# Dealing an expert's third weight matrix to partitions in blocks of four consecutive rows, with a column stride of four in the first product

## The reference

```
def expert_choice_ffn(h, router_w, w1, w3, w2):
    ...
    gate, idx = lax.top_k(aff.T, cap)
    xe = xf[idx]
    hid = jax.nn.silu(jnp.einsum('ecd,edf->ecf', xe, w1)) * jnp.einsum('ecd,edf->ecf', xe, w3)
    ye = jnp.einsum('ecf,efd->ecd', hid, w2) * gate[..., None].astype(h.dtype)
    out = jnp.zeros_like(xf).at[idx.reshape(-1)].add(ye.reshape(-1, D).astype(xf.dtype))
```

## Time and profile before

| | |
|---|---|
| median of 3 runs | 1744.39 us (1741.98 to 1746.46) |
| profiled execution | 1747.4 us |
| its span, first to last instruction | 1745.3 us |
| mean granted TensorE clock over the span | 0.958 |
| PE busy / PEld busy | 1611.5 / 1042.8 us |
| MATMUL at line 1592, both slot sets | 147.4 + 145.4 us busy, 8192 records |
| MATMUL at line 1604, both slot sets | 112.7 + 112.7 us busy, 512 records |

### The profile page before, as it was taken

The page is one execution under the profiler, slowest core; times in us unless marked ns, Lnnn a source line. Parts: engine busy times, 40 slices in busy tenths (PEclk is TensorE's granted clock), DMA queues, the critical chain, the costliest instruction groups (busy, mean ns, idle before and its releaser), DMA issues.

```text
span 1745.3 us, 38027 instructions
## 1 busy us (share of the span) xinstructions
PE 1611.5 (92%) x16782; PEld 1042.8 (60%) x16782; DVE 614.0 (35%) x1286; ACT 430.5 (25%) x726; POOL 248.3 (14%) x251
## 2 busy tenths in 40 slices
PE   5999989999869999999999989888888978999997
PEld 2554435655447677666655467667765546676764
DVE  4543584641520000003149456644463151110110
ACT  3245414530411111103010246432231032100000
POOL 0000000000001111100000036155540001121211
PEclk9999999999989999998999989999899998999998
DMA  9635444031589999973211100011114226999995
GB/s 341 206 129 192 145 151 103 1 145 48 213 309 365 383 389 391 379 284 132 85 61 52 48 1 2 1 51 51 51 51 169 85 109 220 379 379 378 396 388 182
DMA packets 89167, 324.84 MB, mean 186 GB/s; under 512 B 10836, under 2 KB 16584, under 8 KB 80872
## 3 DMA queue, kind: packets, MB, share of 16 engines
q1 hardware_dynamic: 75296, 284.67, 43.1%
q0 software_dynamic: 9456, 32.65, 6.9%
q10 hardware_dynamic: 4312, 6.03, 1.0%
HBM read 301.17 MB, written 22.16 MB: 185 GB/s over the span
## 4 chain that ended last, share of the span: by engine, by line
PE 72%; DVE 6%; DMA 4%; issue 3%; ACT 1%; POOL 0%; POOLq 0%; ACTq 0%; DVEq 0%; SPq 0%
PE pairs L223 19%; PE pairs L1592 15%; PE pairs L1604 12%; PE pairs L1575 2%; PE pairs L1236 2%; PE pairs L345 2%; DMA ring<-in_exp_w 2%; PE pairs L1250 1%; PE pairs L2074 1%; PE pairs L2301 1%; PE pairs L2094 1%; PE pairs L2057 1%; PE pairs L2312 1%; DMA ring<-in_w_mod 1%; PE pairs L734 1%
## 5 line engine op out<-in xcount | busy, mean ns | idle before, releaser
L223 PE MATMUL pairs<-hT,ring 128*128 128x128 f32 (+1 forms) x1120 | 306.1, 435 | 2.2 <-ACT hT L359 2.2
L223 PEld LDWEIGHTS pairs<-hT,ring 128*128 128x128 f32 x1120 | 170.3, 192 | 138.5 <-issue 138.4
L359 ACT ACTIVATE arena<-pairs 128x512 f32<-128x512 f32 (+6 forms) x212 | 124.0, 603 | 393.5 <-PE pairs L223 126.5
L223 PE MATMUL pairs<-ring,hT 128*128 128x512 f32 (+1 forms) x448 | 178.5, 557 | 0.0
L1592 PEld LDWEIGHTS pairs<-arena 128*64 128x64 f32 x4096 | 144.5, 138 | 14.4 <-issue 14.3
L1592 PEld LDWEIGHTS pairs<-arena,ring 128*64 128x64 f32 x4096 | 142.7, 137 | 13.9 <-issue 13.9
L1592 PE MATMUL pairs<-arena 128*64 128x80 f32 x4096 | 147.4, 234 | 2.5 <-issue 1.5
L1592 PE MATMUL pairs<-arena,ring 128*64 128x80 f32 x4096 | 145.4, 233 | 0.9 <-issue 0.9
L223 PEld LDWEIGHTS pairs<-ring,hT 128*128 128x128 f32 x448 | 84.4, 190 | 90.1 <-issue 87.1
L1604 PE MATMUL pairs<-arena 128*80 128x512 f32 x256 | 112.7, 592 | 1.5 <-issue 1.5
L1604 PE MATMUL pairs<-ring,arena 128*80 128x512 f32 x256 | 112.7, 593 | 0.2 <-DMA ring<-in_exp_w 0.2
(11 more groups left out here) (398 smaller groups left out, 2141.4 us busy)
## 6 DMA issues: line engine op xcount, KB each, us to landing
arena<-in_exp_w SPq DMA_DIRECT2D x48, 2048.0 KB, 19.1
ring<-in_exp_w SPq DMA_DIRECT2D x48, 2048.0 KB, 20.2
ring<-in_w_mod SPq DMA_DIRECT2D x24, 2048.0 KB, 8.1
ring<-in_w_in_ab SPq DMA_DIRECT2D x5, 2048.0 KB
ring<-in_w_in_cd SPq DMA_DIRECT2D x5, 2048.0 KB, 10.4
ring<-in_w_out SPq DMA_DIRECT2D x4, 2048.0 KB, 21.6
h_rows<-arena POOLq DMA_DIRECT2D x2, 2560.0 KB, 10.1
arena<-moe_rows ACTq DMA_DIRECT2D x4, 640.0 KB, 6.7
```

The lines of the kernel that those rows point to most:

```text
L223: last = pe.matmul(out, lhs(k), rhs(k), start=(k == 0), stop=(k == KD - 1))
L359: return eng.activation(dst, src, ACT.Copy) if eng is nc.scalar else eng.tensor_copy(dst, src)
```

## The change

w2 is laid out as w1 and w3 are: partition p gets rows 4p to 4p+3, one piece of 16 KB. Block f of w2 on partition p is then row 4p+f. So the first product takes, for block f, the columns f, f+4, f+8, ... of w1 and w3: its stationary operand is 64 elements that lie 16 bytes apart on each partition instead of 64 neighbours. The numbers of instructions and all shapes on TensorE, VectorE, ScalarE and GpSimd stay, and their order too. The moving operands (`xeT`, w2) are read as before.

```diff
-        W2 = [io["exp_w2"][l].rearrange("e (k p) d -> p (e k) d", p=P) for l in range(2)]
+        W2 = [io["exp_w2"][l].rearrange("e (p k) d -> p e (k d)", p=P) for l in range(2)]
...
-                                last = pe.matmul(lin_of(j, f)[c:c + 64, :], w[:, k, f * P + c:f * P + c + 64], rhs,
+                                last = pe.matmul(lin_of(j, f)[c:c + 64, :], w[:, k, f + FT * c:FT * (c + 64):FT], rhs,
                                                  start=(k == 0), stop=(k == KD - 1))
...
             w = (W1, W3, W2)[j][l]
-            if j == 2:
-                dst, src = slots[s].rearrange("p (k n) -> p k n", n=D), w[:, bass.ds(i * FT, FT), :]
-            else:
-                dst, src = slots[s].unsqueeze(1), w[:, bass.ds(i, 1), :]
-            sp.dma_start(dst, src).then_inc(w_here[s], 16)
+            sp.dma_start(slots[s].unsqueeze(1), w[:, bass.ds(i, 1), :]).then_inc(w_here[s], 16)
```

## The result

The changed kernel takes 1940.86 us, the median of 4 runs (1937.82 to 1944.86). The kernel before took 1743.18 us beside it. The ratio is 1.1146 with a 95% interval of 1.1096 to 1.1197: **198 us slower**, where 1744 was forecast and the range ended at 1915.

A forecast was written before the change was run, and what follows sets the result against it. TensorE's chain was taken as the bound, transfers just behind. Terms: -0.3 us (w2 in time) + 0.3 (first gather) + 0 (strided weights) = 0, so 1744.39 stays 1744 us; range 1738 to 1915.

The forecast's parts named there:

- What bounds the kernel: Expert stages: TensorE on the chain, busy 268.17 of 269 us at full clock; transfers, 0.99 and 0.97 busy, just reach the deadline.
- The load of w2: w2 transfers: larger pieces save 0.11 us an expert and remove line 1604's wait; gain 0.3 us, at most 0.5.
- The pauses without a releaser: Layer 1: TensorE pauses four times with no releaser, 3.95 us in all, perhaps hanging on busy transfer engines.
- one of its rivals: Transfers as the bound: shorter w2 loads give 3.5 us, vanished pauses 4, so 1737 us; chance 0.05.
- The first gather: Layer 0's first gather: w2's larger pieces hold it back, 0.3 us taken, 2.3 at most.
- The strided weights: Line 1592: 64 strided columns load in 54 ns, under the 69.6 of a pair, so cost 0.
- second price, 1.8 times: Line 1592: the stride multiplies an ordinary load as a transpose, 96 ns for 64 columns; loss 108 us, time 1852.
- the rival: Slow weights at line 1592: a half's load needs over 69.6 ns; 1850 to 1915 us, chance 0.32.
- The upper end: Line 1592: shared limit and the 211 ns records' streamed rate together, 111 ns a pair, 1914 us.
- two halves with a shared limit: Line 1592: both halves' loads share one limit, 107 ns a pair instead of 69.6; loss 153 us, time 1897.
- the prediction's last paragraph: Profile after: if first product nears 13.7 us, the failed step took 0.84 ns a column as one load's limit, not the pair's.

The follow-up runs named there:

- experiment 1: The changed kernel's w2 load, with the first product's neighbouring columns of the kernel before: 1743.04 us against 1737.87, ratio 1.0016.
- experiment 2: The changed kernel's first product with columns strided by four, w2 in four pieces as in the kernel before: 1942.19 us, ratio 1.1161.
- experiment 3: The kernel before, each block of 128 hidden units as one matmul with 128 neighbouring weight columns instead of two halves: 1913.18 us, one run.
- experiment 4: The changed kernel, each block of 128 hidden units as one matmul with 128 columns strided by four instead of two halves: 2453.28 us, one run.
- experiment 6: The kernel before, with the first product's 64 weight columns three elements (12 bytes) apart: 1818.8 us, one run.
- experiment 7: The kernel before, with the first product's 64 weight columns eight elements (32 bytes) apart, the halves taking neighbouring columns: 1950.29 us, one run.
- experiment 10: The kernel before, weights unchanged, with the first product's moving operand strided, 80 elements of xeT 16 bytes apart: 2029.39 us, one run.
- experiment 5: The kernel before, with w2 in two pieces of 8 KB a partition and the first product taking every second column: 1741.92 us, ratio 1.0006.
- experiment 8: The kernel before, with ScalarE writing h's rows so that line 1575's transposes take 128 neighbouring columns: 1742.79 us, ratio 1.0022.

## Why the prediction was wrong

**What bounds the kernel** was right: TensorE on the chain, at full clock, transfers just behind. What the weight loads lost went straight to the end.

**The load of w2**, gain 0.3 us: right as far as it can be read. The wait of line 1604 for w2 is gone in experiment 1 and the ratio there is 1.0016 (0.9992 to 1.0041). The pauses without a releaser, which the prediction tied to busy transfer engines in one of its rivals, are absent from the profiles of the changed kernel and of experiments 2, 3, 4, 6, 7 and 10, where an expert takes longer and the transfers have slack. They stay where the transfers are near their limit: 3.95 us before, 7.0 in experiment 1, 2.6 in experiment 5. That fits the rival's cause and doesn't prove it. Whether larger pieces lengthen them isn't shown by one profile each.

**The first gather**, 0.3 us taken, 2.3 at most: mis-sized. It measured 1.9 us, near the upper end.

**The strided weights**, taken as 0: this failed. The room was right, 69.6 ns for a pair and 1.09 ns a column; experiment 6, at 89.4 ns for 48 lines, shows that it is overrun well before a stride of four. The failed step is: "If the limit is one access of a strided column in 0.84 ns for each load, 64 columns take 54 ns". The row for 0.84 ns was a transpose. I carried its absolute rate over to an ordinary float32 load, whose contiguous rate happened to be the same, and took that as room. The ratio was what carried over: a contiguous transpose takes 0.45 ns a column and a strided one 0.86, an ordinary load 0.83 and 1.75 (experiments 3 and 4): 1.9 times and 2.1 times. The 0.45 is the prediction's figure from a record's length. Eight contiguous transposes in a row (experiment 8) came every 77 ns, which gives no more than 0.60 as an upper end, so the first ratio is a rough one. The prediction had that reading as its second price, 1.8 times, and had it too small. It took the stride's factor from the first, unqueued load of a series (185 ns) and left out the fixed part, and so came to 96 ns where 120.5 were measured. That is why 1852 to 1914 for the rival fell short of 1941. The upper end has a slip of its own: the prediction doesn't say how records of 211 ns make 111 ns a pair. By its own formula they give (211 - 83)/128 = 1.00 ns a column, 128 ns a pair and 1983 us. That end would have covered 1941 by luck, since it rests on the shared limit that experiment 4 refutes.

The other reading of the rival, two halves with a shared limit, is refuted by experiment 4. It named the right place with the wrong mechanism, and so did the prediction's last paragraph, which in case of a loss would have blamed a limit of the pair. What the prediction took from the Trainium skill, "TensorE: Matmul & The Clock Gate", section "Step-by-step: what each phase is for", that column halves have read interfaces of their own, agrees with experiment 4: 120.5 ns for both halves, 232.5 for one load of 128 columns. The halves share no limit here; the interfaces themselves are in no trace. It wasn't enough, since each half was slow by itself.

**The granted clock** played no part in what the weights cost. Why an ordinary load takes twice as long for a line as a transpose isn't settled. That it reads each element twice would fit both its rates, contiguous and strided, but no run shows it.

The clock does explain why the profiled span grew by 190.4 us when the expert stages grew by 202. Between the stages, in layer 1's mixer, the same work took 12 us less. The windows before, then after the change:

```profile
1005.00:1336.00 331.00, 288.08 (x4708) 224.97 (x4708) 173.04 (x331) 125.09 (x250) 143.87 (x156) 0.93 0.09 30
```

```profile
1109.00:1428.00 319.00, 275.87 (x4707) 217.16 (x4706) 173.11 (x331) 125.13 (x250) 143.70 (x156) 0.97 0.09 30
```

The other engines are busy for the same time, TensorE for 12 us less at a granted clock of 0.97 instead of 0.93, and 288.08 x 0.93/0.97 is 276. The kernel before varies in this way by itself: its runs lie between 1730 us, with a mean granted clock of 0.971, and 1748, with 0.958. Its profile was taken at 1747.4, near the slow end, and that of the changed kernel at 1937.82, the fastest of its four runs.

## What to carry to other kernels

In this kernel TensorE read float32 weights from SBUF at their old pace only while each 16-byte line was used twice: a step of two elements was free, three cost 28% on this product, four 73% and eight 75%. A step of four in the moving operand cost as much an element; two and three weren't tried there. A layout that makes a transfer's pieces larger wasn't worth a stride of four on TensorE. Pieces of 4 KB already ran at 417 GB/s against 426 for 16 KB. And when a price is carried from one kind of instruction to another, work it out both ways, by its absolute rate and by its ratio to its own contiguous form, and keep the dearer one as the other end. Here the ratio was nearer.

## What the runs showed that was not expected

The strided loads don't follow TensorE's clock. In experiment 4 a load of 128 columns came every 232.5 ns while the granted clock went from 2.4 to 1.2 GHz, and the contiguous ones of experiment 3 came every 214 ns at 1.2 GHz and every 111 at 2.4.

The chip granted less clock while the array waited for weights: experiment 4 had a mean granted clock of 0.784, against 0.958 for experiment 3, which issues the same instructions. The strided product lost nothing by it, since its loads set the pace. The second product behind it did, by about 49 us.
